# Half a step ahead instead of two slabs: when the weight sums of a Winograd MLP are queued

## The chip, the cores and the metric

The kernel runs on 8 cores of one Trainium2 chip, one batch row a core, with no exchange between cores. The metric is device time in microseconds (us) of the slowest core. The engines are named as in the profile: PE (matrix products), PEld (its weight loads), DVE (vector engine), ACT (scalar engine), POOL (GpSimd, which here issues the weight DMAs), SP (which issues the other DMAs).

## The reference

Two layers, each a token mixer and a squared-ReLU MLP with a residual add, then a final RMSNorm. x is (8, 2048, 1024) in float32.

```python
for i in range(2):
    h = rmsnorm(x, norm_mix_g[i])
    x = x + (mlstm_mixer if i == 0 else gla_mixer)(h, ...)   # chunkwise, 4 heads, chunks of 64
    h = rmsnorm(x, norm_ffn_g[i])
    x = x + square(relu(h @ ffn_w1[i])) @ ffn_w2[i]          # 1024 -> 4096 -> 1024
return rmsnorm(x, final_norm_g)
```

The change concerns the two MLPs and how their weights are prepared.

## The kernel before

Every core keeps its row of x transposed in SBUF (`xT`, 8 x 128 channels by 2048 tokens in four groups of 512) and runs in this order: mLSTM mixer, MLP of layer 0 (FFN0, some 300 to 700 us), GLA mixer, MLP of layer 1 (FFN1, from some 970 us), final norm and stores.

**The MLP.** Class `Ffn` works in steps. An "up" step makes 4 x 128 hidden columns for a pair of token groups and uses one *slab* of w1, a "down" step brings a pair of output blocks and uses two slabs of w2. A slab is 1024 x 256 weights, 1 MiB in float32, written as bf16 into one of six slots; 64 slabs a layer. Except in some last steps the product is Winograd's 2 x 2 scheme: seven block products instead of eight (1, 5, 6, 2, 3, 7, 4, in this order; `prod`), for which sums of weight blocks are needed. `Ffn.sums` makes them on DVE, four instructions a slab by `sum16` (L276): `wsum_0`, `wsum_1`, one in place in the slab, and `wsum_2`. Product 5 reads wsum_0, 6 wsum_1, 7 the sum in place and 3 wsum_2; products 1, 2 and 4 read the raw slab. An up step is 28 matmuls of 512 columns (L254), a down step 56.

**Names.** The slots' raw slabs are wraw_68, 69, 70, 71, 72 and 73 for slots 0, 1, 2, 3, 4 and 5; their first sums are wsum_0_76, 79, 82, 85, 88 and 91. In listings of orders the same tiles are wraw0_68, wsum0_0_76 and so on. `rt` or `tmp` <- `ps` at L272 (custom add-and-relu; "ISA" in listings of orders) is the eviction of products 3 and 7 out of a PSUM bank `ps`; PE can't start a product in that bank before. `Ffn.load` issues a slab's DMA on POOL's queue (L211) once PE and DVE have read the slot's last slab for the last time, which is the *gate*.

**Ticks.** While a step's products are recorded, `tick` is called after product 2 and after product 3; it runs one waiting piece of other work (`due`: norms, squares, loads of the next stage).

**What sets the order.** Instructions are not emitted as recorded. Class `Trk` records them as units with a modelled duration, and `Trk.order` simulates all engines with a list scheduler: at each step it takes, within a window of the next 48 (PE, ACT, DVE), 24 (POOL) or 4 (SP) recorded units of an engine, the one that the model can start first, the earliest recorded where several can. A DMA's landing in that model is `done[n]`, from its size and a fixed lateness; the same numbers never reach the chip. The emitted order of each engine is fixed, and semaphores hold it: an engine waits at the head of its queue.

`Ffn.run` calls `s.sums(upto)` at the start of a step, which records the sums of all slabs below `upto` that have been recorded as loaded.

Of the kernel before, what the change touches and what calls it, by code (L numbers as in the profile page):

```python
# [28 lines left out]
class Trk:  # L29
# [55 lines left out]
    def order(s):  # L85
        lastw, readers = {}, {}
        for n, u in enumerate(s.units):
            preds = set()
            for k in u["r"]:
                if k in lastw:  # L90
                    preds.add(lastw[k])
            for k0 in u["w"]:
                for k in s.ov(k0):
                    if k in lastw:
                        preds.add(lastw[k])
                    preds.update(readers.get(k, ()))
            preds.discard(n)
            u["preds"] = preds
            for k in u["r"]:
                readers.setdefault(k, []).append(n)  # L100
            for k in u["w"]:
                lastw[k] = n
                readers[k] = []
        todo = {e: [n for n, u in enumerate(s.units) if u["eng"] == e] for e in s.E}
        free = {e: 1500.0 for e in s.E}
        done, seq, hbm, xq = {}, [], 0.0, 0.0
        best = {e: None for e in s.E}
        dirty = set(s.E)
        while any(todo.values()):
            for e in s.E:  # L110
                best[e] = None
                cand = []
                held = False
                for n in todo[e][:s.WIN[e]]:
                    if s.units[n]["dma"]:
                        if held:
                            continue
                        held = True
                    rdy = 0.0
                    for p in s.units[n]["preds"]:  # L120
                        d = done.get(p)
                        if d is None:
                            rdy = None
                            break
                        pe = s.units[p]["eng"]
                        if pe == e == "pe":
                            d -= 163
                        elif s.units[p]["dma"] is None:
                            d += 206 if pe == "pe" and e == "act" else s.HOP[e]
                        rdy = max(rdy, d)  # L130
                    if rdy is None:
                        continue
                    st, safe = max(free[e], rdy), max(free[e], rdy + s.SLACK)
                    cand.append((safe, n, st))
                    if safe <= free[e]:
                        break
                if cand:
                    t0 = min(cand)[0]
                    best[e] = min((n, st) for safe, n, st in cand if safe <= t0 + 20)
            e = min((b[1], e) for e, b in best.items() if b is not None)[1]  # L140
            n, st = best[e]
            u = s.units[n]
            todo[e].remove(n)
            free[e] = st + (u["ns"] if u["dma"] else max(u["ns"] - max(s.LEAD[e], 0), 60))
            if u["dma"] and u["xp"]:
                free[e] = st + 1300
                pk = 64 if u["xp"] == "hn" else 32
                b = max(st + 1000, xq)
                slow = min(pk, int(max(0.0, hbm - b) / 200))
                xq = b + slow * 200 + (pk - slow) * 18  # L150
                done[n] = xq + 950
            elif u["dma"]:
                hbm = max(hbm, st + 1500) + u["dma"][1] / 0.29e3
                done[n] = hbm + (1200 if st < 60000 else 2500)
            else:
                done[n] = st + u["ns"] - min(s.LEAD[e], 0)
            u["st"] = st
            seq.append(n)
        s.model = max(done.values())
        return seq  # L160
# [67 lines left out]
def build():  # L228
# [22 lines left out]
    t = Trk(nc, es)  # L251
# [29 lines left out]
    def at(name, shape, dt, off=None):  # L281
        n = int(np.prod(shape[1:])) * (4 if dt == F32 else 2)
        if off is None:
            off = cur[0]
            cur[0] += (n + 31) // 32 * 32
        return nc.alloc_sbuf_tensor_at(name, list(shape), dt, offset=off), off
# [24 lines left out]
    wraw = [at("wraw%d" % i, [128, 8, 2, 128], BF16, o[0])[0] for i, o in enumerate(slots)]  # L311
# [135 lines left out]
    def nb(keep=False, full=False):  # L447
        for n in range(16):
            ring["i"] = (ring["i"] + 1) % len(ring["banks"])
            a = ring["banks"][ring["i"]]  # L450
            if a not in ring["open"] and (not full or a in ring["full"]):
                break
        else:
            assert full
            a = nb()
            mm(PB[a][:], ones_bf[:], sqb[:], [("sqb",), ("ones_bf",)], [("B", a)], True, True, True, 512)
            ring["full"].add(a)
        if keep:
            ring["open"].add(a)
        if not full:  # L460
            ring["full"].discard(a)
        return a
# [99 lines left out]
    def stats_slots(g, eng="pool"):  # L562
        return [lambda: sq_half(g, 0, eng), lambda: sq_half(g, 1, eng), lambda: sq_sum(g)]
# [14 lines left out]
    class Ffn:  # L578
# [22 lines left out]
        def load(s, gate=()):  # L601
            sl = s.slabs[s.nload]
            s.nload += 1
            i = sl["slot"]
            t.dma("pool", [(wraw[i][:].rearrange("p k a n -> p k (a n)"), sl["src"])], 1048576, r=gate,
                  w=[("wr", i), ("w3", i)], sem="slab%d" % i)

        def loads(s, used):
# [198 lines left out]
            s.loads(st["slabs"][0] - 1)  # L807

        def tick(s):
            if s.due:  # L810
                s.due.pop(0)()

        def run(s, n0, n1, hooks, late=()):
            late = list(late)
            for n in range(n0, n1):
                st = s.steps[n]
                fns = s.due = list(hooks.get(n, []))
                if n > n0 and st["kind"] != s.steps[n - 1]["kind"] or not st["wino"]:
                    for fn in late:
                        fn()  # L820
                    late = []
                    s.loads(st["slabs"][0] - 1)
                assert s.nload > st["slabs"][-1]
                s.sums(st["slabs"][-1] + 3)
                if not st["wino"]:
                    for fn in s.up_std(st)[st["done"]:]:
                        fn()
                        s.tick()
                else:
                    late = (s.up_wino if st["kind"] == "up" else s.down_wino)(st, late)  # L830
                while fns:
                    s.tick()
                s.loads(st["slabs"][0] - 1)
                if not late:
                    s.loads(st["slabs"][-1])
            for fn in late:
                fn()
            s.loads(s.steps[n1 - 1]["slabs"][-1])
# [407 lines left out]
    for k0 in range(0, KC, 2):  # L1246
        load_cols(wqk, "wqk", m_win_d, 0, 1, ks=(k0, k0 + 1))
        if k0 < 4:
# [6 lines left out]
         r=[("tri_f",)], w=[("tri_f",)], ns=400)  # L1255
# [163 lines left out]
    for k in range(KC):  # L1419
        i, n = ((1, 11 + k), (2, k - 2), (3, k - 5))[(k > 1) + (k > 4)]  # L1420
# [33 lines left out]
    for g in range(2):  # L1454
        st = stats_slots(g, "dve")
# [24 lines left out]
    for (c0, n), bank, queues in zip(PARTS, (6, 7, 5), (("sp", "sp"), ("pool", "pool"), ("sp", "act"))):  # L1480
        ts = slice(g * GS + c0, g * GS + c0 + n)
        for j in range(KC):
            a = nb()
# [5 lines left out]
            if c0:  # L1489
                t.op("pool", lambda e, j=j, ts=ts: e.tensor_scalar(  # L1490
                    out=xT[:, j, ts], in0=xT[:, j, ts], scalar1=gains[:, 32 + j:33 + j], scalar2=None, op0=ALU.mult),
                    r=[("gains",)], w=[("xT", j, g, c0)], ns=450)
# [56 lines left out]
```

How the kernel before makes its waits and increments, by code:

```python
    def _waits(s, ename, reads, writes):  # L162
        e = s.E[ename]
        pesem = s.E["pe"]["sem"]
        need = {}
        def add(sem, val):
            if ename == "pe" and sem is pesem:
                return
            if need.get(sem, 0) < val:
                need[sem] = val
        for k in reads:
            t = s.lastw.get(k)
            if t:
                add(*t)
        for k0 in writes:
            for k in s.ov(k0):
                t = s.lastw.get(k)
                if t:
                    add(*t)
                for sem, val in s.readers.get(k, {}).items():
                    add(sem, val)
        for sem, val in need.items():
            if e["waited"].get(sem, 0) < val:
                e["eng"].wait_ge(sem, val)
                e["waited"][sem] = val
# [10 lines left out]
    def emit(s):  # L197
# [11 lines left out]
                for o, i in u["dma"][0]:  # L209
                    c += 16
                    (e["eng"].dma_start_transpose if u["xp"] else e["eng"].dma_start)(out=o, in_=i).then_inc(sem, 16)
                if name:
# [15 lines left out]
def build():  # L228
# [1265 lines left out]
                act(xT[:, j, ts], xT[:, j, ts], AF.Identity, [("gains",)], [("xT", j, g, c0)], n,  # L1494
                    scale=gains[:, 32 + j:33 + j])
            if due and j > 1:
                due.pop(0)()
        rstd_fin(bank, c0, n)
        due += out_part(g, c0, n, bank, queues)
    for fn in due:
        fn()
    t.emit()
    for u in toks:
        nc.sync.wait_ge(*u["tok"])
    es.close()
    mybir.codegen_inst_isa_subclasses(nc)
    return nc
```

## Time and profile before

| | |
|---|---|
| median of 6 runs | 1381.95 us (1379.12 to 1433.39) |
| profiled execution | 1381.22 us |
| span of its slowest core | 1380.2 us |
| spans of all cores | 1372.3 to 1380.2 us, granted clock 0.990 to 0.997 |
| PE busy, slowest core | 1327.6 us, 96% |
| DVE busy | 955.8 us, 69% |
| slab DMAs and others on POOL's queue | 91.92 MB, 48.9% of the DMA engines' time |

Busy time is the union of an engine's instructions over the span. PE is the engine to look at: what it is not busy with is what another engine or a DMA can win or lose for it, so the waits of PE, and the waits of the engine that it waits for, are the views to read.

### The profile page before, as it was taken

The page shows a single profiled execution, that of the slowest core. Times are in us where ns is not written, and L with a number is a line of the kernel's source. Part 1 is how long each engine was busy: PE and PEld are TensorE (multiplying, and loading weights), DVE is VectorE, ACT ScalarE, POOL GpSimd, SP SyncE. Part 2 cuts the span into 40 slices and gives each one's busy share as a digit, 9 for nine tenths or more (in the row PEclk, how much of TensorE's full clock was granted, in tenths as well). Part 3 has the DMA queues.
Part 4 walks back from the last instruction along what each step waited for, and adds up shares of the span by engine and source line. Part 5 has one row for each costly group of instructions (what it writes and reads, how often), then busy time and mean ns, then how long its engine had stood idle before and what let it go on. Part 6 is the DMA issues. An engine that isn't in the chain of part 4 may idle for free.

```text
span 1380.2 us, 23130 instructions; the slowest of 8 cores (1372.3 to 1380.2 us)
## 1 busy us (share of the span) xinstructions
PE 1327.6 (96%) x6813; PEld 625.8 (45%) x6813; DVE 955.8 (69%) x2088; ACT 753.1 (55%) x1606; POOL 233.4 (17%) x263
## 2 busy tenths in 40 slices
PE   5999999899999999999999999999999999998997
PEld 2555554443444444444444545444444444443445
DVE  2498384967568977567658866677665888886836
ACT  2486665637158266176238765664452953942565
POOL 6021111211111111112012002050111111111114
PEclk9999999999999999999999999999999999999998
DMA  9945111368577596758674201034747857778853
GB/s 164 240 100 113 37 32 24 51 71 105 72 97 92 61 108 81 92 62 105 103 147 105 47 16 32 16 43 62 91 63 93 107 75 90 95 124 133 103 71 123
DMA packets 202011, 118.86 MB, mean 86 GB/s; under 512 B 53872, under 2 KB 187168, under 8 KB 201888
## 3 DMA queue, kind: packets, MB, share of 16 engines
q0 software_dynamic: 143392, 91.92, 48.9%
q1 hardware_dynamic: 57968, 25.20, 8.6%
q8 instruction: 57, 0.93, 0.3%
q14 instruction: 66, 0.54, 0.2%
q10 hardware_dynamic: 528, 0.26, 0.1%
HBM read 176.46 MB, written 8.39 MB: 134 GB/s over the span
## 4 chain that ended last, share of the span: by engine, by line
PE 82%; DMA 8%; DVE 4%; issue 3%; ACT 1%; POOL 1%; SPq 0%; DVEq 0%; ACTq 0%; POOLq 0%
PE ps L254 82%; DMA wraw_69<-w 2%; DMA wqk<-m_win 1%; DMA wraw_70<-w 1%; DMA wraw_72<-w 1%; DMA wraw_68<-w 1%; DMA wraw_73<-w 1%; DVE xT L264 0%; DMA xT<-m_wout 0%; DVE Cbf L1112 0%; DVE NB L988 0%; DVE R_110 L268 0%; DVE rt L272 0%; SPq L211 0%; ACT og_112 L260 0%
## 5 line engine op out<-in xcount | busy, mean ns | idle before, releaser
L260 ACT ACTIVATE ps<-ps 128x512 f32<-128x512 f32 x184 | 106.3, 584 | 190.9 <-PE ps L254 163.0
L264 DVE TENSOR_TENSOR xT<-ps,xT 128x512 f32<-128x512 f32 (+2 forms) x224 | 142.3, 647 | 95.2 <-PE ps L254 94.9
L260 ACT ACTIVATE rt<-ps 128x512 f32<-128x512 f32 x156 | 91.5, 590 | 94.1 <-PE ps L254 92.1
L260 ACT ACTIVATE sq<-xT 128x512 f32<-128x512 f32 x128 | 78.6, 626 | 29.2 <-DVE sd L264 11.6
L268 DVE SCALAR_TENSOR_TENSOR R_110<-R_110,egs,ps 128x256 f32<-128x256 f32 x112 | 52.8, 471 | 14.4 <-PE ps L254 13.4
L260 ACT ACTIVATE junk<-ps 128x256 bf16<-128x256 f32 x128 | 49.0, 383 | 25.3 <-DVE ps L264 14.2
L264 POOL TENSOR_TENSOR sd<-sd,sq 128x512 f32<-128x512 f32 x40 | 51.1, 1278 | 37.4 <-ACT sq L260 30.1
L264 POOL TENSOR_TENSOR sd<-sq 128x512 f32<-128x512 f32 x8 | 10.3, 1288 | 275.0 <-ACT sq L260 266.9
L211 POOL DMA_DIRECT2D wraw_68<-w x23 | 20.2, 878 | 196.5 <-PE ps L254 81.4
L1112 DVE TENSOR_SCALAR Cbf<-R_110,egs 128x256 bf16<-128x256 f32 x120 | 46.7, 423 | 0.9
L272 DVE CUSTOM_DVE_ANT_0 rt<-ps,rt 128x512 f32<-128x512 f32 x43 | 29.4, 685 | 22.0 <-PE ps L254 22.0
L254 PE MATMUL ps<-xn_44,wqk 128*128 128x512 bf16 x128 | 31.8, 399 | 12.6 <-DMA wqk<-m_win 12.2
L211 POOL DMA_DIRECT2D wraw_73<-w x22 | 19.3, 877 | 129.7 <-PE ps L254 69.6
L260 ACT ACTIVATE og_112<-og_112 128x512 f32<-128x512 f32 x60 | 37.6, 628 | 3.7 <-ACT og_112 L260 0.8
L211 POOL DMA_DIRECT2D wraw_69<-w x21 | 18.5, 879 | 123.0 <-PE ps L254 52.0
L260 ACT ACTIVATE og_113<-og_113 128x512 f32<-128x512 f32 x60 | 37.7, 630 | 2.7
L211 POOL DMA_DIRECT2D wraw_70<-w x19 | 16.7, 879 | 109.8 <-PE ps L254 70.8
L988 DVE TENSOR_TENSOR_SCAN NB<-ones_bf,NB 128x128 f32<-128x128 bf16 x64 | 25.4, 440 | 13.8 <-ACT NB L260 12.6
L211 POOL DMA_DIRECT2D wraw_71<-w x20 | 17.6, 880 | 99.3 <-PE ps L254 26.5
L254 PE MATMUL ps<-xn_46,wout 128*128 128x512 bf16 x128 | 29.9, 379 | 2.3 <-DVE xs_55 L268 1.3
L254 PE MATMUL ps<-wo,xn_44 128*128 128x512 bf16 x128 | 31.6, 395 | 0.0
L254 PE MATMUL ps<-xn_44,wout 128*128 128x512 bf16 x128 | 30.8, 389 | 0.8 <-ACT tiny L260 0.6
(842 smaller groups left out, 3602.0 us busy)
## 6 DMA issues: line engine op xcount, KB each, us to landing
wraw_68<-w POOLq DMA_DIRECT2D x23, 512.0 KB, 7.1
wraw_73<-w POOLq DMA_DIRECT2D x22, 512.0 KB, 7.8
wraw_69<-w POOLq DMA_DIRECT2D x21, 512.0 KB, 7.3
wraw_72<-w POOLq DMA_DIRECT2D x21, 512.0 KB, 7.6
wraw_71<-w POOLq DMA_DIRECT2D x20, 512.0 KB, 6.7
wraw_70<-w POOLq DMA_DIRECT2D x19, 512.0 KB, 8.2
outT<-xT SPq DMA_DIRECT2D x12, 512.0 KB, 6.6
xT<-xT POOLq DMA_DIRECT2D x6, 512.0 KB, 31.7
```

The costliest lines, as they stand in the source:

```text
L211: (e["eng"].dma_start_transpose if u["xp"] else e["eng"].dma_start)(out=o, in_=i).then_inc(sem, 16)
L254: t.op("pe", lambda e: e.matmul(out, lhsT=lhsT, rhs=rhs, start=start, stop=stop, **kw), r=r, w=w, sig=sig, ns=max(cols, 64) * (1.7 if f32 ...
L260: t.op("act", lambda e: e.activation(out=out, in_=in_, func=func, **kw), r=r, w=w, ns=190 + 0.84 * n + (80 if acc is not None else 0))
L264: t.op(eng, lambda e: e.tensor_tensor(out=out, in0=in0, in1=in1, op=op), r=r, w=w, ns=170 + 1.03 * n if eng == "dve" else 200 + 2.2 * n)
L268: t.op("dve", lambda e: e.scalar_tensor_tensor(out=out, in0=in0, scalar=scalar, in1=in1, op0=op0, op1=op1), r=r, w=w, ns=200 + 1.07 * n)
L272: t.op("dve", lambda e: e._custom_dve(dve_ops.TENSOR_ADD_SAT, out=out, in0=in0, in1=in1, s0=3.0e38, s1=0.0), r=r, w=w, ns=170 + 1.03 * n)
L988: t.op("dve", lambda e, cv=cv: e.tensor_tensor_scan(out=cv, data0=ones_bf[:], data1=cv, initial=0.0, op0=ALU.mult, op1=ALU.add), r=[("ones ...
L1112: t.op("dve", lambda e, h=h: e.tensor_scalar(out=Cbf[:, h, :], in0=R32[:, h, :], scalar1=ec[:, h:h + 1], scalar2=None, op0=ALU.mult), r=[( ...
```

## The change

Sums are recorded later, and the scheduler's model is told other numbers. At the start of a Winograd step only the sums up to that step's own last slab are recorded (`+1`; before, two slabs further, `+3`). The slabs of the next step are put in `s.ahead`, and each tick records the sums of one of them, ahead of the tick's other piece of work. In the model a slab's transfer takes 1150000 instead of 1048576 bytes' time, and a DMA with its own slab semaphore lands 4000 ns instead of 2500 after its modelled transfer when it starts after 60 us.

```diff
--- before.py
+++ after.py
@@ -151,7 +151,7 @@
                 done[n] = xq + 950
             elif u["dma"]:
                 hbm = max(hbm, st + 1500) + u["dma"][1] / 0.29e3
-                done[n] = hbm + (1200 if st < 60000 else 2500)
+                done[n] = hbm + (1200 if st < 60000 else 4000 if u["sem"] else 2500)
             else:
                 done[n] = st + u["ns"] - min(s.LEAD[e], 0)
             u["st"] = st
@@ -602,7 +602,7 @@
             sl = s.slabs[s.nload]
             s.nload += 1
             i = sl["slot"]
-            t.dma("pool", [(wraw[i][:].rearrange("p k a n -> p k (a n)"), sl["src"])], 1048576, r=gate,
+            t.dma("pool", [(wraw[i][:].rearrange("p k a n -> p k (a n)"), sl["src"])], 1150000, r=gate,
                   w=[("wr", i), ("w3", i)], sem="slab%d" % i)
 
         def loads(s, used):
@@ -807,6 +807,8 @@
             s.loads(st["slabs"][0] - 1)
 
         def tick(s):
+            if s.ahead:
+                s.sums(s.ahead.pop(0) + 1)
             if s.due:
                 s.due.pop(0)()
 
@@ -821,7 +823,8 @@
                     late = []
                     s.loads(st["slabs"][0] - 1)
                 assert s.nload > st["slabs"][-1]
-                s.sums(st["slabs"][-1] + 3)
+                s.sums(st["slabs"][-1] + (1 if st["wino"] else 3))
+                s.ahead = list(s.steps[n + 1]["slabs"]) if st["wino"] and n + 1 < len(s.steps) else []
                 if not st["wino"]:
                     for fn in s.up_std(st)[st["done"]:]:
                         fn()
```

What this does to the emitted orders is shown at three places.

DVE at the start of FFN0, where slot 0's slab 6 and slot 1's slab 7 are summed. d_50 and d_51 are the semaphores of the slabs of slots 0 and 1; hid are hidden columns, whose squares and sums are made here. Before; the evictions of ps5 and ps6 stand three and four rows below the last row:

```order
L276 TENSOR_TENSOR wsum0_0_76<-wraw0_68 128x512 [waits d_50]
L272 ISA rt_121<-ps1,rt_121 128x512 [waits s_pe]
L276 TENSOR_TENSOR wsum0_1_77<-wsum0_0_76,wraw0_68 128x512 [waits s_dve]
L276 TENSOR_TENSOR hid2_62<-hid2_62 128x512 [waits s_act]
L272 ISA rt_121<-ps2,rt_121 128x512 [waits s_pe]
L276 TENSOR_TENSOR wraw0_68<-wraw0_68 128x4x128
L276 TENSOR_TENSOR wsum0_2_78<-wraw0_68,wsum0_1_77 128x512 [waits s_dve]
L276 TENSOR_TENSOR hid3_63<-hid3_63 128x512 [waits s_act]
L276 TENSOR_TENSOR wsum1_0_79<-wraw1_69 128x512 [waits d_51]
L276 TENSOR_TENSOR hid3_63<-hid3_63 128x512 [waits s_dve]
L276 TENSOR_TENSOR wsum1_1_80<-wsum1_0_79,wraw1_69 128x512 [waits s_dve]
L276 TENSOR_TENSOR wraw1_69<-wraw1_69 128x4x128
```

After; the eviction of ps1 stands two rows ahead of the first row:

```order
L272 ISA rt_121<-ps2,rt_121 128x512 [waits s_pe]
L276 TENSOR_TENSOR wsum0_0_76<-wraw0_68 128x512 [waits d_50]
L276 TENSOR_TENSOR hid3_63<-hid3_63 128x512 [waits s_act]
L276 TENSOR_TENSOR wsum0_1_77<-wsum0_0_76,wraw0_68 128x512 [waits s_dve]
L276 TENSOR_TENSOR wraw0_68<-wraw0_68 128x4x128
L276 TENSOR_TENSOR hid3_63<-hid3_63 128x512 [waits s_dve]
L276 TENSOR_TENSOR wsum0_2_78<-wraw0_68,wsum0_1_77 128x512 [waits s_dve]
L276 TENSOR_TENSOR hid3_63<-hid3_63 128x512 [waits s_dve]
L276 TENSOR_TENSOR hid3_63<-hid3_63 128x512 [waits s_act,s_dve]
L272 ISA rt_121<-ps5,tmp1_123 128x512 [waits s_pe]
L276 TENSOR_TENSOR wsum1_0_79<-wraw1_69 128x512 [waits d_51]
L272 ISA rt_121<-ps6,tmp1_123 128x512 [waits s_pe]
```

The first sum of slot 0 stood ahead of the evictions of ps1 and ps2, and now stands behind both; the first sum of slot 1 stood ahead of the evictions of ps5 and ps6 and now stands between them.

PE at the start of the GLA mixer, with its projections (wv, wqk, wo) and the small gate product z = zl x wgu. Before:

```order
L254 MATMUL ps7<-wv_49,xn2_46 128x512 [waits s_act]
L254 MATMUL ps7<-wv_49,xn2_46 128x512 x7
L254 MATMUL ps0<-wv_49,xn2_46 128x512 [waits s_act]
L254 MATMUL ps0<-wv_49,xn2_46 128x512 x7
L254 MATMUL ps7<-xn3_47,wqk_48 128x512 [waits s_act]
L254 MATMUL ps7<-xn3_47,wqk_48 128x512 x7
L254 MATMUL ps1<-zl_118,wgu_128 128x512 [waits s_dve]
L254 MATMUL ps2<-zl_118,wgu_128 128x512 [waits s_dve]
L254 MATMUL ps0<-xn3_47,wqk_48 128x512 [waits s_act]
L254 MATMUL ps0<-xn3_47,wqk_48 128x512 x7
```

After:

```order
L254 MATMUL ps2<-wo_50,xn2_46 128x512 [waits s_dve]
L254 MATMUL ps2<-wo_50,xn2_46 128x512 x7
L254 MATMUL ps0<-wv_49,xn2_46 128x512 [waits s_act]
L254 MATMUL ps0<-wv_49,xn2_46 128x512 x7
L254 MATMUL ps7<-xn3_47,wqk_48 128x512 [waits s_act]
L254 MATMUL ps7<-xn3_47,wqk_48 128x512 x7
L254 MATMUL ps0<-xn3_47,wqk_48 128x512 [waits s_act]
L254 MATMUL ps0<-xn3_47,wqk_48 128x512 x7
L254 MATMUL ps1<-zl_118,wgu_128 128x512 [waits s_dve]
L254 MATMUL ps2<-zl_118,wgu_128 128x512 [waits s_dve]
```

The z matmuls stand behind one more block of eight wqk matmuls.

DVE in FFN1 by the output stage, where the multiplies of finished token groups (xT <- xT, gains, ps7 at L268, `out_held`) lie between sums; d_53 and d_55 are the slab semaphores of slots 3 and 4. Before:

```order
L276 TENSOR_TENSOR wsum3_0_85<-wraw3_71 128x512 [waits d_53]
L268 SCALAR_TENSOR_TENSOR xT_43<-xT_43,gains_131,ps7 128x512 [waits s_dve]
L276 TENSOR_TENSOR wsum3_1_86<-wsum3_0_85,wraw3_71 128x512 [waits s_dve]
L276 TENSOR_TENSOR wraw3_71<-wraw3_71 128x4x128
L268 SCALAR_TENSOR_TENSOR xT_43<-xT_43,gains_131,ps7 128x512 [waits s_dve]
L276 TENSOR_TENSOR wsum3_2_87<-wraw3_71,wsum3_1_86 128x512 [waits s_dve]
L276 TENSOR_TENSOR wsum4_0_88<-wraw4_72 128x512 [waits d_55]
L268 SCALAR_TENSOR_TENSOR xT_43<-xT_43,gains_131,ps7 128x512 [waits s_dve]
L276 TENSOR_TENSOR wsum4_1_89<-wsum4_0_88,wraw4_72 128x512 [waits s_dve]
L276 TENSOR_TENSOR wraw4_72<-wraw4_72 128x4x128
L268 SCALAR_TENSOR_TENSOR xT_43<-xT_43,gains_131,ps7 128x512 [waits s_dve]
L276 TENSOR_TENSOR wsum4_2_90<-wraw4_72,wsum4_1_89 128x512 [waits s_dve]
```

After:

```order
L268 SCALAR_TENSOR_TENSOR xT_43<-xT_43,gains_131,ps7 128x512 [waits s_dve]
L276 TENSOR_TENSOR wsum3_1_86<-wsum3_0_85,wraw3_71 128x512 [waits s_dve]
L276 TENSOR_TENSOR wraw3_71<-wraw3_71 128x4x128
L268 SCALAR_TENSOR_TENSOR xT_43<-xT_43,gains_131,ps7 128x512 [waits s_dve]
L276 TENSOR_TENSOR wsum3_2_87<-wraw3_71,wsum3_1_86 128x512 [waits s_dve]
L268 SCALAR_TENSOR_TENSOR xT_43<-xT_43,gains_131,ps7 128x512 [waits s_dve]
L276 TENSOR_TENSOR wsum4_0_88<-wraw4_72 128x512 [waits d_55]
L268 SCALAR_TENSOR_TENSOR xT_43<-xT_43,gains_131,ps7 128x512 [waits s_dve]
L276 TENSOR_TENSOR wsum4_1_89<-wsum4_0_88,wraw4_72 128x512 [waits s_dve]
L276 TENSOR_TENSOR wraw4_72<-wraw4_72 128x4x128
L276 TENSOR_TENSOR wsum4_2_90<-wraw4_72,wsum4_1_89 128x512 [waits s_dve]
```

The first sum of slot 4 stands one multiply later, and the last multiply right behind it instead of behind two more sums and a multiply.

## Rows read from the trace of the kernel before

**Rows 1.** The cores: the slowest core and the next to it.

```profile
core 0: 1380.2 us, clock 0.993
...
core 2: 1380.1 us, clock 0.994
```

**Rows 2.** The page: busy time of each engine, slowest core.

```profile
PE 1327.6 (96%) x6813; PEld 625.8 (45%) x6813; DVE 955.8 (69%) x2088; ACT 753.1 (55%) x1606; POOL 233.4 (17%) x263
```

**Rows 3.** Stretches: length, PE, PEld, DVE, ACT, POOL, PEclk, DMA share, GB/s.

```profile
350.00:640.00 290.00, 286.97 (x1328) 129.37 (x1325) 205.05 (x443) 154.94 (x285) 42.04 (x50) 1.00 0.67 83
640.00:700.00 60.00, 59.97 (x275) 26.35 (x275) 40.30 (x83) 16.81 (x30) 8.91 (x12) 1.00 0.75 107
```

**Rows 4.** PE's waits, 300 to 700 us: in total, times, longest.

```profile
PE ps L254 <- DVE rt L272: 4.4, 4, 2.5
PE ps L254 <- DVE tmp_122 L272: 1.6, 1, 1.6
```

**Rows 5.** PE's waits, 970 to 1370 us: in total, times, longest.

```profile
PE ps L254 <- DVE xT L268: 3.4, 1, 3.4
PE ps L254 <- DVE rt L272: 2.1, 2, 1.0
PE ps L254 <- DMA wraw_71<-w: 1.9, 1, 1.9
...
PE ps L254 <- DMA wraw_69<-w: 0.6, 1, 0.6
```

**Rows 6.** Timeline, 298 to 330 us: start, length, engine, line, instruction [idle before].

```profile
301.89 0.88 POOL L211 DMA_DIRECT2D wraw_72<-w  x1 [18.04 <-PE ps L254]
...
303.62 0.90 POOL L211 DMA_DIRECT2D wraw_69<-w  x1
...
311.70 0.43 DVE L276 TENSOR_TENSOR wsum_0_88<-wraw_72 128x512 bf16<-128x512 bf16 x1 [2.75 <-DMA wraw_72<-w]
...
315.91 0.43 DVE L276 TENSOR_TENSOR wsum_0_76<-wraw_68 128x512 bf16<-128x512 bf16 x1 [1.31 <-DMA wraw_68<-w]
...
316.25 0.68 DVE L272 CUSTOM_DVE_ANT_0 rt<-ps,rt 128x512 f32<-128x512 f32 x1
...
318.35 1.02 PE L254 MATMUL ps<-xs_59,wraw_71 128*128 128x512 bf16 x4 [2.46 <-DVE rt L272]
...
320.37 0.43 DVE L276 TENSOR_TENSOR wsum_0_79<-wraw_69 128x512 bf16<-128x512 bf16 x1 [0.92 <-DMA wraw_69<-w]
...
323.94 1.02 PE L254 MATMUL ps<-xs_59,wraw_73 128*128 128x512 bf16 x4 [0.77 <-DVE rt L272]
```

**Rows 7.** Timeline of DVE and of PE, 602 to 609 us.

```profile
606.60 0.43 DVE L276 TENSOR_TENSOR wsum_0_76<-wraw_68 128x512 bf16<-128x512 bf16 x1 [0.56 <-DMA wraw_68<-w]
606.94 0.68 DVE L272 CUSTOM_DVE_ANT_0 tmp_122<-ps,rt 128x512 f32<-128x512 f32 x1
...
607.77 1.02 PE L254 MATMUL ps<-xs_59,wraw_70 128*128 128x512 bf16 x4 [1.61 <-DVE tmp_122 L272]
```

**Rows 8.** Timeline by the output stage, 1238 to 1262 us: POOL, DVE, PE.

```profile
1239.66 0.88 POOL L211 DMA_DIRECT2D wraw_72<-w  x1
...
1255.83 0.43 DVE L276 TENSOR_TENSOR wsum_0_88<-wraw_72 128x512 bf16<-128x512 bf16 x1 [5.25 <-DMA wraw_72<-w]
...
1257.51 0.74 DVE L268 SCALAR_TENSOR_TENSOR xT<-xT,gains,ps 128x512 f32<-128x512 f32 x1
...
1258.39 0.38 PE L254 MATMUL ps<-hid_60,wsum_0_79 128*128 128x512 bf16 x1 [3.45 <-DVE xT L268]
```

**Rows 9.** Timeline of PE, 1336 to 1341 us.

```profile
1338.74 1.02 PE L254 MATMUL ps<-xs_59,wraw_70 128*128 128x512 bf16 x4 [1.05 <-DVE rt L272]
```

**Rows 10.** Timeline of PE at the start of the GLA mixer.

```profile
735.46 1.13 PE L254 MATMUL ps<-zl,wgu 16*128 16x512 f32 x4
...
743.93 3.61 PE L254 MATMUL ps<-xn_47,wqk 128*128 128x512 bf16 x16 [0.52 <-DVE qx_151 L268]
```

**Rows 11.** DVE's waits for slabs, whole span: costliest and least of six.

```profile
DVE wsum_0_88 L276 <- DMA wraw_72<-w: 15.8, 8, 5.3
...
DVE wsum_0_91 L276 <- DMA wraw_73<-w: 5.2, 7, 1.3
```


## The prediction

> **What bounds the kernel now.** I read the cores first, then the page's busy times, then what TensorE (PE) waits for, and last the timeline at each such wait. The profiled execution took 1381.22 us; its slowest core spans 1380.2, so 1.0 lies around the span, and it stands 0.7 below the median of 1381.95. Core 2 is only 0.1 shorter [rows 1], so a gain that holds on core 0 alone counts for nothing. PE is busy 96% of the span and no other engine more than 69% [rows 2]. In a quiet stretch of FFN0, 350 to 640 us, PE works 286.97 of 290 us at the full granted clock, 216 ns a 512-column matmul [rows 3]. So a change of order cannot win much: it can only take away PE's own waits, and PE is idle for 1380.2 − 1327.6 = 52.6 us in all.
>
> The waits that belong to weight slabs are few. From 300 to 700 us PE waits five times, 6.0 us, for the relu eviction (L272) [rows 4]. From 970 to the end it waits 3.4 for the output stage's L268, 2.1 for L272 and 2.5 for two slabs themselves [rows 5]. Two things in the rows say why an *eviction* is late:
>
> - Place A, 316 us. Three loads are issued 0.87 us apart, the first at 301.89, and their first sums run at 311.70, 315.91 and 320.37, each after VectorE (DVE) had waited for the DMA. The eviction of 316.25 stands right behind the second; PE then starts at 318.35, 2.46 late, and 0.77 late again after the third [rows 6].
> - Place D, 607 us. The sum at 606.60 waited for its slab; the eviction starts at 606.94, on its heels, and PE runs at 607.77, 1.61 late [rows 7].
>
> In the first listing of DVE's order above, wsum0_0 of slot 0 stands ahead of the evictions of ps1 and ps2, which PE had long filled. DVE runs in order, so a late slab holds two finished banks, and PE stops for lack of a bank, not for lack of a weight.
>
> At place F, by the output stage, the same thing happens with the last multiply of a group: the sum at 1255.83 waited 5.25 us for its slab, the multiply started at 1257.51 behind it, and PE at 1258.39, 3.45 late [rows 8].
>
> **The change, part by part.** It adds and removes no instruction: SP's order is the same, and POOL's differs by one mixer weight load. Nothing of a slab's DMA changes on the chip either; 1150000 and 4000 are numbers of the scheduler's model. So the price of work is 0 and everything comes from who stands behind whom.
>
> *Sums later.* In the order after, wsum0_0 stands behind both evictions of its step. The evictions then go when PE has filled their banks. What this gives, wait by wait:
>
> - A: 2.46 + 0.77 = 3.23 [rows 6]. The sum at 311.70 stays ahead of them, and wsum1_0 now stands between the evictions of ps5 and ps6, so some stays. Without the wait of the second sum, the eviction at 316.25 could go 1.31 (that wait) and 0.43 (the sum) sooner, and the second one another 0.43 (wsum0_1, which stood between): 2.17 of 2.46. Of the 0.77 I take a little: **2.3** in all.
> - B and C, two smaller ones of the same form (411 and 505 us): the L272 row of 300 to 700 has 4.4 in four, less A's 3.23, is 1.17 [rows 4, 6]: **1.1**.
> - D: the sum that waits has gone from ahead of the eviction: **1.6** [rows 7].
> - E, 984 to 993 us: PE waits 0.6 for a slab itself and once about 1.0 for L272 [rows 5]. Of the two L272 waits there, one (1338.74) has no sum near it and stays [rows 9]. The slab's load goes out sooner in the order after by several matmuls, since the wait that stalled its gate is gone: **1.6**.
> - F: 1.9 for a slab [rows 5] and 3.45 for the multiply [rows 8]. Behind the waiting sum the order after has the last multiply at once; before, one multiply and two sums stood between, 1257.51 − 1255.83 = 1.68 from the sum's start, of which 0.34 remains. That gives 1.3, and PE asks for the result two matmuls (0.4) later: 1.7. The first load is also gated 7 matmuls (1.5 us) earlier, which would give up to 1.5 more if the transfer used it. Bounds 1.7 to 3.2; I take **2.0**, near the low one, because the transfer that ends the wait runs beside output stores and took 16 us, from 1239.66 to 1255.8 [rows 8].
>
> Sum: 2.3 + 1.1 + 1.6 + 1.6 + 2.0 = **8.6**.
>
> *The cost.* DVE's sums now come nearer to their use. Counted in the orders, the shortest distance from the eviction ahead of a sum to PE's first use of it was 29 matmuls and is 14, at three places; the median falls from 85 to 77. 14 × 0.216 = 3.0 us against four sums at 0.43 [rows 6] = 1.7: cover is left, 1.3 us of it at the tightest place. I take 0. Without that cover, the three places would cost at most what the largest slab wait here cost, 3.45 each.
>
> The mixer that follows is ordered anew as well, because the model's times have moved. The four z matmuls (zl, wgu) stand one 8-matmul block later, as the second fence of orders shows; they start the chain of gates that ends in the wait of 743.93, 0.52 us today [rows 10]. A block of eight is 8 × 0.216 = 1.7. If the chain slips by 1.7 and PE's own work in front of that wait is unchanged, the wait grows by up to 1.7; the block itself isn't lost, since PE does it anyhow. Bounds: 0 (other work fills it) and 4 (the stretch 640 to 700, where PE is busy 59.97 of 60 [rows 3], opens gaps of its own as well). I take **1.5**.
>
> Net −8.6 + 1.5 = −7.1: 1381.2 − 7.1 = 1374.1 for the profiled execution, and with the 0.7 to the median **1374.8**.
>
> **A rule weighed.** Whether the slabs' transfers could be the bound themselves: at A three loads land 4.2 and 4.5 us apart [rows 6], and PE needs 28 × 0.216 = 6.05 for the products of a slab [rows 3], so transfers have a third in hand; the DMA engines are 0.67 busy there [rows 3], which says the same.
> The Trainium skill, DMA: Bandwidth & Descriptors, section Bandwidth, lists 6.15 us (341 GB/s) for a transfer of 1 MB issued from GpSimd. By that figure a slab would take longer than its products, PE would follow the transfers, and the change would save nothing. The trace's spacing of 4.2 to 4.5 us differs from it, and the measurement decides.
>
> **The rivals.**
>
> 1. *The waits are the transfers', and slip along.* Loads are gated by PE's last use of a slot, so an earlier PE asks earlier, but the DMA lands when it can. A's spacing of 4.2 to 4.5 in bursts speaks for it, and the 16 us of F; the third in hand speaks against. The stalls stay, the mixer costs 1.5: 1381.95 + 1.5 = **1383.5**. 0.15.
> 2. *More goes away.* F loses all 5.3 instead of 2.0, A all 3.2, and the mixer costs nothing: −8.6 − 3.3 − 0.9 = −12.8, **1369.2**. For it: F's wait is a queue behind one sum, and the order after shortens it on both sides. 0.15.
> 3. *Half of it.* F keeps its waits and the mixer costs 4: −6.6 + 4 = −2.6, **1379.3**: not told from no change. 0.11.
> 4. *Slower: a sum now stands between two evictions.* Place: the listing after, wsum1_0 between the evictions of ps5 and ps6, in each step that has such a pair. DVE waits for slabs 50 times, 62.2 us, six groups of which the costliest and the least are shown [rows 11]; of that 12.9 reaches PE (3.23 + 1.17 + 1.6 + 1.6 + 5.3, A to F), about a fifth. If 30% got through, 18.7, PE would lose 5.8 more and 1.5 in the mixer: 1381.95 + 7.3 = **1389.2**. It decides from 15.5 us (12.9 + 4.1 − 1.5), a quarter of the 62.2. Against it: the second eviction's bank is asked for later, and the sum that stood ahead of both has gone. 0.09.
>
> **How the numbers follow.** The forecast, 1374.8, gets 0.50; the rivals 0.15, 0.15, 0.11 and 0.09. About 0.3%, 4.1 us, is what a measurement of this kernel can tell from no change: faster is below 1377.8, slower above 1386.1. Faster: the forecast and rival 2, 0.65. Same: rivals 1 and 3, 0.26, of which 0.01 at rival 1's upper end goes to slower: 0.25. Slower: 0.09 + 0.01 = 0.10. The likeliest case's own range is 1372 to 1377.5, from F's bounds (−1.2) and the mixer's (−1.5 to +2.5). The range of 8 in 10 takes in rivals 2 and 3: **1368.5 to 1381.5**, leaving out rival 1's upper half and rival 4.
>
> **What would show it.** Right: PE's waits for L272 from 300 to 700 fall from 6.0 to about 1; the wait for L268 by the output stage falls below 2; DVE's waits for slabs remain in sum, but no longer with an eviction behind them; the mixer's wait at 743.93 grows to about 2; cores 2 and 3 shorten by as much as core 0. Wrong: PE waits on sums (L276), which today it doesn't; PE's waits for slabs themselves grow; or the span from 640 to 970 lengthens by more than 4.

## The result and the profile after

The changed kernel takes 1375.77 us (median of 10 runs) against 1382.47 for the kernel before (20 runs): a ratio of 0.9939, interval 0.9916 to 0.9963. The medians are of all executions, while ratios, means and the ranges of single executions leave out those in which the cores of a die ran at a lower granted clock, so a ratio isn't that of the two medians. The forecast was 1374.8. The profiled execution took 1374.1 us; its cores are these (span, granted clock):

```profile
core 0: 1364.9 us, clock 0.995
core 1: 1373.0 us, clock 0.993
core 2: 1368.6 us, clock 0.995
core 3: 1362.1 us, clock 0.997
```

Core 0, the slowest before [rows 1], is 15.3 us shorter; the slowest is now core 1. Which core is the slowest changes from execution to execution, so one core says little: the mean of the eight (the mean core, further on) went from 1376.9 us to 1367.7. The profiled execution before was a poor one in this respect; over all executions beside e1 to e4 the mean core before is 1374.1. The page of core 1 has for the engines:

```profile
PE 1327.5 (97%) x6813; PEld 627.1 (46%) x6813; DVE 956.1 (70%) x2088; ACT 756.4 (55%) x1606; POOL 234.0 (17%) x263
```

PE's busy time on the slowest core is the same to 0.1 us [rows 2]; there the gain is idle time. From the first to the last matmul on a slab of each layer, as a mean over eight cores, FFN0 went from 431.3 to 428.8 us, the GLA mixer between them from 245.3 to 246.5, and FFN1 from 425.3 to 417.9. So both MLPs gave, and the mixer took something back, more than these numbers say: one more block of eight wqk matmuls of the mixer (1.7 us) now runs ahead of FFN0's last slab matmul (173 matmuls that use no slab against 165), so some 1.7 us are FFN0's gain and the mixer's loss. In FFN1 the mean granted clock rose as well, from 0.994 to 1.000.

PE's waits from 300 to 700 us, and below them those from 970 to 1370 (total, times, longest):

```profile
PE ps L254 <- DVE rt L272: 1.1, 2, 0.7
PE ps L254 <- DVE xT L264: 0.3, 1, 0.3
...
PE ps L254 <- DMA wraw_70<-w: 2.1, 1, 2.1
PE ps L254 <- DVE rt L272: 1.4, 2, 1.0
```

The 6.0 us of late evictions in FFN0 [rows 4] are 1.1, and the wait for the output stage's multiply, 3.4 [rows 5], is gone. At place A the timeline of core 1 reads:

```profile
301.84 0.88 POOL L211 DMA_DIRECT2D wraw_72<-w  x1 [18.03 <-PE ps L254]
...
312.03 0.42 DVE L276 TENSOR_TENSOR wsum_0_88<-wraw_72 128x512 bf16<-128x512 bf16 x1 [1.34 <-DMA wraw_72<-w]
...
313.71 0.68 DVE L272 CUSTOM_DVE_ANT_0 rt<-ps,rt 128x512 f32<-128x512 f32 x1
314.65 0.68 DVE L272 CUSTOM_DVE_ANT_0 rt<-ps,rt 128x512 f32<-128x512 f32 x1
315.25 0.41 DVE L276 TENSOR_TENSOR wsum_0_76<-wraw_68 128x512 bf16<-128x512 bf16 x1
315.47 1.02 PE L254 MATMUL ps<-xs_59,wraw_71 128*128 128x512 bf16 x4 [0.49 <-DVE rt L272]
...
320.30 0.43 DVE L276 TENSOR_TENSOR wsum_0_79<-wraw_69 128x512 bf16<-128x512 bf16 x1 [0.84 <-DMA wraw_69<-w]
320.64 0.68 DVE L272 CUSTOM_DVE_ANT_0 rt<-ps,tmp_123 128x512 f32<-128x512 f32 x1
321.47 1.02 PE L254 MATMUL ps<-xs_59,wraw_73 128*128 128x512 bf16 x4 [0.66 <-DVE rt L272]
```

The loads go out within 0.1 us of those of [rows 6] and the sums of the second and third slab run at about the same time; but both evictions stand ahead of wsum_0_76, and PE loses 0.49 where it lost 2.46. The sum of slot 1 still lies ahead of an eviction and costs 0.66.

DVE's waits for slabs, whole span (two of seven rows):

```profile
DVE wsum_0_91 L276 <- DMA wraw_73<-w: 4.4, 5, 1.5
...
DVE wsum_0_88 L276 <- DMA wraw_72<-w: 1.7, 2, 1.3
```

All seven sum to 17.2 us, against the 62.2 of six rows in [rows 11]; in the mean of the eight cores, 60.8 us became 14.9. That was not forecast: DVE now comes to most sums when the slab is there.

### The profile page after: what moved, and what is told of

Same layout as the page of the kernel before. It is cut to its first block, busy times and chain, and to the rows that moved or that the text cites. A ratio compares the mean times of both kernels' runs of the same rounds, so it can differ in the third digit from the quotient of the medians.

```text
span 1373.0 us, 23119 instructions; the slowest of 8 cores (1362.1 to 1373.0 us)
## 1 busy us (share of the span) xinstructions
PE 1327.5 (97%) x6813; PEld 627.1 (46%) x6813; DVE 956.1 (70%) x2088; ACT 756.4 (55%) x1606; POOL 234.0 (17%) x263
## 4 chain that ended last, share of the span: by engine, by line
PE 88%; DMA 4%; DVE 3%; issue 3%; ACT 1%; POOL 1%; DVEq 0%; ACTq 0%; POOLq 0%; SPq 0%
PE ps L254 88%; DMA wqk<-m_win 2%; DMA wraw_69<-w 1%; DMA wraw_70<-w 1%; DVE Cbf L1115 1%; DVE R_110 L268 0%; DVE NB L991 0%; DVE xT L264 0%; DMA xn_44<-hn 0%; DVE hn L268 0%; POOL wqk L211 0%; POOL xT L1493 0%; ACT og_112 L260 0%; DVE xs_52 L268 0%; DVE ps L264 0%
## 5 line engine op out<-in xcount | busy, mean ns | idle before, releaser
L260 ACT ACTIVATE sq<-xT 128x512 f32<-128x512 f32 x128 | 78.7, 627 | 35.2 <-DVE sd L264 17.2
L268 DVE SCALAR_TENSOR_TENSOR R_110<-R_110,egs,ps 128x256 f32<-128x256 f32 x112 | 52.8, 472 | 18.5 <-PE ps L254 17.5
L211 POOL DMA_DIRECT2D wraw_68<-w x23 | 20.2, 877 | 201.1 <-PE ps L254 82.1
L1115 DVE TENSOR_SCALAR Cbf<-R_110,egs 128x256 bf16<-128x256 f32 x120 | 49.5, 445 | 1.2 <-PE ps L254 0.3
L211 POOL DMA_DIRECT2D wraw_73<-w x22 | 19.3, 878 | 120.5 <-PE ps L254 73.5
L211 POOL DMA_DIRECT2D wraw_69<-w x21 | 18.5, 879 | 117.8 <-PE ps L254 48.5
L211 POOL DMA_DIRECT2D wraw_70<-w x19 | 16.7, 878 | 111.5 <-PE ps L254 81.5
L211 POOL DMA_DIRECT2D wraw_71<-w x20 | 17.7, 886 | 97.4 <-PE ps L254 25.3
L211 POOL DMA_DIRECT2D wraw_72<-w x21 | 18.5, 880 | 76.5 <-PE ps L254 18.0
```

Of the source, the lines that this page charges most:

```text
L211: (e["eng"].dma_start_transpose if u["xp"] else e["eng"].dma_start)(out=o, in_=i).then_inc(sem, 16)
L260: t.op("act", lambda e: e.activation(out=out, in_=in_, func=func, **kw), r=r, w=w, ns=190 + 0.84 * n + (80 if acc is not None else 0))
L268: t.op("dve", lambda e: e.scalar_tensor_tensor(out=out, in0=in0, scalar=scalar, in1=in1, op0=op0, op1=op1), r=r, w=w, ns=200 + 1.07 * n)
L1115: t.op("dve", lambda e, h=h: e.tensor_scalar(out=Cbf[:, h, :], in0=R32[:, h, :], scalar1=ec[:, h:h + 1], scalar2=None, op0=ALU.mult), r=[( ...
```

## The experiments

Theory M: the model's later landings place the sums, whatever lead they are recorded with. Its rival S: the recording half a step ahead does it, as the change is worded. A third theory, L, is on where the time goes: all that the change wins back is what late slabs cost in front of evictions.

**One edit alone.** e1 takes the model's numbers back in the changed kernel:

```diff
-                done[n] = hbm + (1200 if st < 60000 else 4000 if u["sem"] else 2500)
+                done[n] = hbm + (1200 if st < 60000 else 2500)
-            t.dma("pool", [...], 1150000, r=gate,
+            t.dma("pool", [...], 1048576, r=gate,
```

> The changed kernel with the model's two old numbers (1048576 bytes, 2500 ns); only the recording of sums half a step ahead is left of the change. Theory M (the model's numbers carry the gain: the list scheduler places the sums by their modelled landing, whenever they were recorded): no change from before, 1382.5 within 0.3% (1378 to 1386.5), DVE's waits for slabs near 62 us on the slowest core, PE's slab waits near 13 us. Theory S (the later recording carries the gain, as the change is worded): near the changed kernel, 1375.8 within 3.

Measured: 1389.39 us, ratio 1.0038, interval 1.0017 to 1.0060; slower than before by 0.4%, which neither theory had. The mean over cores and executions is what it was (1374.5, before 1374.1), but the slowest core averages 1386.4 against 1380.6. In its profile, core 0:

```profile
PE ps L254 <- DVE rt L272: 9.0, 7, 2.5
PE ps L254 <- DMA wraw<-w: 3.8, 1, 3.8
```

DVE waits 56.2 us for slabs there. The late evictions are still there, and one slab is later for PE itself. S falls. Why the slowest cores went beyond before isn't settled: the executions at 1387 to 1391 weren't the profiled one; their slowest cores show granted clocks of 0.989 to 0.993.

e2 is the other half, the kernel before with the two new numbers:

```diff
-                done[n] = hbm + (1200 if st < 60000 else 2500)
+                done[n] = hbm + (1200 if st < 60000 else 4000 if u["sem"] else 2500)
-            t.dma("pool", [...], 1048576, r=gate,
+            t.dma("pool", [...], 1150000, r=gate,
```

> The kernel before with the model's two new numbers (1150000 bytes, 4000 ns for slabs) and sums recorded two slabs ahead as before. Theory M: near the changed kernel, 1375.8 within 3, DVE's waits for slabs below 25 us. Theory S: near before, 1382.5 within 3, DVE's waits for slabs near 62.

Measured: 1379.02 us, ratio 0.9981 (0.9967 to 0.9995): a gain, but a third of the whole; in the mean core, 1371.0 us, it is about half. DVE's slab waits are up to 38.4 us on a core. So M fails here too: it asked for 1378.8 at most and waits below 25. Its slowest core, 6, lost most at one place of its timeline:

```profile
1272.41 0.42 DVE L276 TENSOR_TENSOR wsum<-wraw 128x512 bf16<-128x512 bf16 x1 [6.47 <-DMA wraw<-w]
...
1273.58 3.57 PE L254 MATMUL ps<-xs,wraw 128*128 128x512 bf16 x8 [6.35 <-DVE rt L272]
```

The stretches around it (length, busy times of the engines, PEclk, DMA share, GB/s) are:

```profile
1240.00:1260.00 20.00, 19.07 (x88) 8.50 (x89) 16.50 (x32) 4.53 (x8) 1.78 (x3) 1.00 1.05 177
1260.00:1280.00 20.00, 13.55 (x52) 5.61 (x53) 7.30 (x18) 7.57 (x14) 2.63 (x3) 0.83 0.91 104
```

A sum ahead of an eviction again, at a place where the DMA engines are 0.91 to 1.05 busy, and PE's clock falls behind the wait.

e3 drops the lead altogether in the changed kernel:

```diff
-                s.ahead = list(s.steps[n + 1]["slabs"]) if st["wino"] and n + 1 < len(s.steps) else []
+                s.ahead = []
```

> The changed kernel with no lead in recording at all: the sums of a step's own slabs are recorded at its start and none at its ticks. Theory M: the scheduler still draws them forward within its window, so within 3 us of the changed kernel, 1375.8. Theory S: with half a step less lead PE waits on sums (L276): by product 5, the second of a step; 0.5 us at a third of 116 slabs would be 20 us, so 1385 or more.

Measured: 1374.45 us, ratio 0.9943 (0.9922 to 0.9964), the changed kernel's. So half a step of lead is worth nothing. But e2 and e3 differ in the lead alone, two slabs against none, and their executions don't meet: 1375.6 to 1382.4 us in e2, 1373.3 to 1375.4 in e3, with mean cores of 1371.0 and 1368.6. So recording the sums later gives nothing without the numbers (e1), and with them 2.5 us in the mean core and 4.6 in the median of the slowest: the gain needs both edits.

**How late the model may be.** e4 and e8 change one number of the changed kernel, e8 to 6000 and e4 to 8000:

```diff
-                done[n] = hbm + (1200 if st < 60000 else 4000 if u["sem"] else 2500)
+                done[n] = hbm + (1200 if st < 60000 else 8000 if u["sem"] else 2500)
```

> The changed kernel with 8000 instead of 4000 ns of lateness for slabs in the model. Theory M: the distance from a slab's gate to its deadline grows further, so PE's remaining slab waits (2 to 4 us in the changed kernel) go; the z matmuls of the GLA mixer stand one block earlier again, so its 1.2 us come back: 1372 (1369 to 1375). Rival (sums now too late, PE waits on L276): 1378 or more.

Measured: 1387.26 us, ratio 1.0039 (1.0025 to 1.0053). DVE hardly waits for slabs any more (6.3 us at most on a core), yet FFN0 is 440.5 to 440.8 us long on all cores, 12 more than in the changed kernel, through PE's waits there (265 to 705 us of core 6):

```profile
PE ps L254 <- ACT ps L260: 4.1, 7, 0.9
PE ps L254 <- DVE xT L264: 1.5, 2, 0.9
```

and 16 more mixer matmuls (3.5 us) that were moved ahead into it, by which the mixer got no shorter. The scheduler, told that sums come late, puts PE's products in another order, in which PE waits for ACT's copies of a bank; which products these are wasn't taken apart. Theory M's 1372 was missed by 15 us, and the rival was right in sign, not in its place (L276). The mixer's wait (L996) did not go either, 2.6 to 4.5 us on each core.

> The changed kernel with 6000 instead of 4000 ns of lateness for slabs in the model; with 8000 it was slower than before, through short waits of PE for ACT's copies that stood in all cores alike. If that cost grows evenly with the lateness: 1380 (half way between 4000 and 8000). If it comes only when the sums reach PE's first use: as with 4000 or better, 1372 to 1376.

Measured: 1376.38 us, ratio 0.9922 (0.9896 to 0.9947). Beside e5 to e8 the kernel before averaged 1386.9 us, 5 us more than beside the other runs, for a reason that isn't known, so the ratios of these four are too good; by its time e8 ends within 2 us of the changed kernel (1375.8, later 1374.5). Its cores are more alike: the mean core is 4 us longer (1372.7 against 1368.2 and 1368.8), and in each PE's waits for ACT's copies (0.6 us in the changed kernel) are 4.6. FFN0 is 433.1 to 433.3 us on every core (428.8 in the changed kernel's mean), FFN1 417.1 in the mean (417.9). The cost neither grows evenly nor is it free at 6000.

**Late slabs by themselves.** e5 is the kernel before, e6 the changed one, each with half loads from a layer's seventh slab on, so that both leave out half of these weights; the model's bytes and with them all orders are unchanged:

```diff
+            h = 4 if sl["prev"] >= 0 else 8
-            t.dma("pool", [(wraw[i][:].rearrange("p k a n -> p k (a n)"), sl["src"])], 1048576, r=gate,
+            t.dma("pool", [(wraw[i][:].rearrange("p k a n -> p k (a n)")[:, 0:h], sl["src"][:, 0:h])], 1048576, r=gate,
```

> The kernel before, same orders on every engine, but from the seventh slab of each layer on only half of a slab's weights is loaded (the other half keeps the old contents of the slot), so slabs land early. Theory L (the loss of before is evictions and products held up by late slabs): PE's slab waits of some 13 us on the slowest core go, and with them what the clock loses behind them: 1370 (1367 to 1373). Rival O (the order after is better whenever the slabs land, since evictions stand further ahead): it stays above 1376.

> The changed kernel with the same half loads from the seventh slab of each layer on. Theory L: only what is left of late slabs goes (2 to 4 us), 1371 (1368 to 1374), so nothing is left of the change's gain when both load half, and the kernel before may even be ahead by the mixer's 1 to 2 us. Rival O: faster than the kernel before with half loads by 4 us or more.

Measured: e5 1370.52 us, ratio 0.9885 (0.9855 to 0.9915); e6 1371.67, ratio 0.9890 (0.9862 to 0.9919). The slabs land in 4.3 us at the median of e5, and the two orders end together. So L holds and rival O falls: with slabs in time the order after is worth nothing, and its mean core is 2.0 us behind (1366.6 to 1364.6), which points at the mixer. Half loads also take a third off the bytes of POOL's queue (62.0 of 91.9 MB), so other transfers may gain too; that isn't separated here.

**The mixer.** e7 keeps the changed kernel, but gives the last four slabs of layer 0 the old lateness, so that PE enters the mixer in the order of before:

```diff
-                done[n] = hbm + (1200 if st < 60000 else 4000 if u["sem"] else 2500)
+                done[n] = hbm + (1200 if st < 60000 else u.get("late", 2500))
-                  w=[("wr", i), ("w3", i)], sem="slab%d" % i)
+                  w=[("wr", i), ("w3", i)], sem="slab%d" % i)["late"] = 4000 if s.L or s.nload <= 60 else 2500
```

> The changed kernel, with the model's old 2500 ns for the last four slabs of layer 0 alone. That gives PE the order of before in the GLA mixer's start and leaves both MLPs' orders as after the change. If the mixer's reordering costs what the trace shows (a wait of 2.88 us for the decays, L996, in all cores, where before it waited 0.52 for qx): that wait is gone and the median falls by 1 to 3 us against the changed kernel, 1373 (1371 to 1375). Rival: the mixer's wait only moves to another place, and the median stays at 1375 to 1376.

Measured: 1370.16 us, ratio 0.9875 (0.9839 to 0.9911). That is below its range, but the kernel before took 5 us more than elsewhere there, and the changed kernel wasn't run beside it. e9 to e12 were measured together:

> The changed kernel itself, once more, beside the next three on the same chip: the ratio to before should repeat its 0.994 within 0.002.

> The changed kernel with the model's old 2500 ns for the last four slabs of layer 0, once more. If the mixer's reordering costs the changed kernel its wait of 2.88 us for L996 and what the clock loses behind it: a ratio 0.002 to 0.003 below the changed kernel's, about 0.991. Rival (the first comparison was between chips): the same ratio as the changed kernel, within 0.001.

Measured: the changed kernel (e9) 1374.51 us, ratio 0.9957 (0.9942 to 0.9971), which repeats the first; with the old tail (e10) 1371.26, ratio 0.9921 (0.9897 to 0.9944). The difference of the medians is 3.3 us, that of the mean cores 3.6, and the executions don't meet (1373.6 us and more, 1371.8 and less). In the profiled executions the emitted orders of the two differ from 648 to 757 us alone. In the first profile of the changed kernel, PE's timeline of core 1 has:

```profile
737.09 0.39 PE L254 MATMUL ps<-qT,kT 128*128 128x128 bf16 x4
740.36 0.38 PE L254 MATMUL ps<-vt_105,ktok_102 128*128 128x256 bf16 x2 [2.88 <-DVE egs L996]
```

and its stretches are:

```profile
720.00:740.00 20.00, 17.48 (x95) 8.60 (x93) 14.72 (x36) 15.79 (x44) 2.22 (x4) 1.00 0.44 129
740.00:760.00 20.00, 19.35 (x92) 9.34 (x93) 18.38 (x33) 14.66 (x38) 9.71 (x8) 0.91 0.33 89
```

The same stretches of e10, core 1:

```profile
720.00:740.00 20.00, 19.48 (x103) 9.45 (x102) 14.44 (x38) 16.30 (x44) 1.06 (x2) 1.00 0.35 101
740.00:760.00 20.00, 19.91 (x111) 10.25 (x110) 19.58 (x39) 17.23 (x45) 10.56 (x9) 1.00 0.44 94
```

and of its waits of PE, whole span:

```profile
PE ps L254 <- DVE qx L268: 1.0, 2, 0.5
```

The wait of 2.88 us stands in all eight cores of the changed kernel and in none of e10, where the 0.5 for qx of before is back.

**The lead once more, with the mixer's order held.** e11 is e10 with e3's edit, no lead. e12 is e10 with the lead of before:

```diff
-            if s.ahead:
-                s.sums(s.ahead.pop(0) + 1)
...
-                s.sums(st["slabs"][-1] + (1 if st["wino"] else 3))
-                s.ahead = list(s.steps[n + 1]["slabs"]) if st["wino"] and n + 1 < len(s.steps) else []
+                s.sums(st["slabs"][-1] + 3)
```

> The same with no lead in recording: a step's sums are recorded at its start, none at the ticks. Theory M (with the new numbers the scheduler places the sums itself; half a step of lead in recording is worth nothing): the ratio of the run before it, within 0.001. Theory S: slower by more than 0.003.

> The same with the sums recorded two slabs ahead, as before the change; the mixer's order is the same in all three, so only the lead differs. Theory M alone: the ratio of the two runs before it, within 0.001. If the recording carries a part of its own (without the old tail, the new numbers alone gave 0.998 and both edits 0.994): slower than them by 0.002 to 0.004.

Measured: e11 1371.62 us, ratio 0.9933 (0.9908 to 0.9957); e12 1374.33, ratio 0.9948 (0.9928 to 0.9969). No lead is as good as half a step. Two slabs of lead are worse by 2.7 us in the median and 2.4 in the mean core (1367.5 against 1365.1 for both others), with overlapping intervals. By itself that is only probable; but e2 and e3 gave the same 2.5 in the mean core, and there the executions don't meet.

## Why the prediction was right, and where only by balance

The forecast was −7.1 us, the result −6.7 by the medians (−8.4 by the ratio). Its parts:

- **PE's waits are all there is to win.** Right on the slowest core, where PE's busy time stayed; and with half loads the gain has gone from the comparison (e5, e6). But over the eight cores a part of it is clock: in the two MLPs together PE's idle time fell by 8.7 us in the mean, and what a granted clock below 1.00 costs, worked out as its shortfall times the stretch, by 2.8. The sum had no term for that.
- **A to D.** Right in place and size on the slowest core. 1.15 remains at A (0.49 + 0.66; forecast 0.9), B to D are gone.
- **E.** Wrong on the slowest core: the step that the slab's load goes out sooner, so that PE no longer waits for one. PE now waits for slot 2's slab instead of slot 1's, in the timeline of core 1:

```profile
975.45 0.88 POOL L211 DMA_DIRECT2D wraw_70<-w  x1
...
991.09 0.42 DVE L276 TENSOR_TENSOR wsum_0_82<-wraw_70 128x512 bf16<-128x512 bf16 x1 [2.89 <-DMA wraw_70<-w]
...
988.01 1.02 PE L254 MATMUL ps<-xs_59,wraw_73 128*128 128x512 bf16 x4 [0.34 <-DVE rt L272]
991.13 1.86 PE L254 MATMUL ps<-xs_52,wraw_70 128*128 128x512 bf16 x4 [2.10 <-DMA wraw_70<-w]
```

Four loads are issued within 2.6 us there, as before, and the second took 15.6 us to land (12.1 before, 977.64 to 989.70). Three of the eight cores wait for a slab itself (1.5 to 2.1 us over the span); before, six did (0.9 to 4.1).

- **F.** Too small: I kept 3.3 of 5.3 us because the transfer beside the output stores might not use its earlier gate. The sum that waited 5.25 [rows 8] did not wait:

```profile
1238.09 0.87 POOL L211 DMA_DIRECT2D wraw_71<-w  x1 [7.40 <-PE ps L254]
1240.17 0.87 POOL L211 DMA_DIRECT2D wraw_72<-w  x1 [1.21 <-DVE xT L264]
...
1251.40 0.41 DVE L276 TENSOR_TENSOR wsum_0_88<-wraw_72 128x512 bf16<-128x512 bf16 x1
1251.74 0.74 DVE L268 SCALAR_TENSOR_TENSOR xT<-xT,gains,ps 128x512 f32<-128x512 f32 x1
```

The earlier gate was slot 3's, whose load goes out 1.4 us earlier against PE's work; slot 4's goes out 2.1 us behind it instead of 0.9. But slot 4's slab landed in 8.8 us (7.9 to 9.7 over the cores), where it had taken 16.1 on core 0 and 15.2 on core 2 (10.3 to 12.4 on the others). These two cores alone had waited over 3 us for the multiply. Why the transfer got shorter isn't shown.

- **The sums together.** Forecast −8.6. With the mixer's order of before (e10) the gain is 1381.15 − 1371.26 = 9.9. What the missing 1.3 are made of isn't taken apart: F's 3.3 and E's miss work against each other, and the clock of the first point comes on top.
- **The mixer.** The mechanism was right, the chain of gates starts later, and it ends in a wait; the term was mis-sized, 1.5 for 3.3. The wait that grew is the one for the decays (L996, 2.88), not that for qx (0.52, [rows 10]): 2.4 more. The rest is the clock: from 740 to 760 us five of the eight cores of the profiled execution show a granted clock between 0.91 and 0.97, against 1.00 in all eight before and in e10. On core 1, 0.09 of 20 us is 1.8. Other dips lie elsewhere in the mixer in every run; over the whole mixer and in the mean of the cores, e9 has 2.5 us more of PE's idle time than e10 and 0.9 more lost to the clock, 3.3 together. I had priced a wait at its own length.
- **DVE's waits for slabs remain in sum.** Wrong: 62.2 became 17.2 (see the profile after). A sum that stands later waits less, for its slab lands meanwhile; I had let the wait move with it.
- **Which edit.** The prediction put the new order down to sums being recorded later. That step is wrong: alone it made the kernel slower (e1), and the model's numbers alone gave a third (e2). Both are needed; of the recording it matters that it isn't two slabs ahead (e2 against e3, e12 against e10), not that it is half a step.

Rival 1 fell at A, where the loads went out no sooner and PE yet waited 0.49 instead of 2.46. The 0.67 busy share of the DMA engines held against it there is that of 350 to 640 us; around A (298 to 330) it was 0.85. Rival 2 was true of F, not of the mixer. Rival 4's place exists (0.66 at 321.47) at a quarter of what A cost. So the time was met in part by luck: 1.3 too little at the sums and 1.8 too little at the mixer nearly cancel.

The best kernel of the study is the changed one with the old tail (e7, e10): 0.9921 of before and, side by side, 3.3 us under the changed kernel.

## What to carry to other kernels

In a queue that runs in order, an instruction that waits for a transfer is priced by what stands behind it: look first for a finished bank that cannot be evicted, not for a product that lacks its weights. Where a scheduler sets the order, its assumed landing time is a tuning knob that can be set too early and too late: too early puts such waits ahead of evictions, too late bends the order of the engine that bounds (with the sums recorded late, 2500 ns gave 1.004 of before, 4000 gave 0.994, 8000 gave 1.004), and every turn also reorders stages that it was not meant for, so look at those. Try two edits that act on one order together as well as apart. When the time is that of the slowest of eight cores, look at the mean as well: e1 had the mean of before and a slowest core 6 us longer, e8 nearly the slowest core of the changed kernel and a mean 4 us longer.

## What the runs showed of the hardware

A wait of PE can cost more than its length. Behind the 6.35 us at 1273.58 in e2, eight matmuls took 3.57 us, some 0.43 each where 0.216 is usual, which is the lower of the clock's two levels; the granted clock of that stretch was 0.83. Behind the 2.88 us wait in the mixer the clock fell in five cores of eight and stayed in three, with the same instructions ahead of it in all of them; in e9, five of eight again, but not the same five. The same transfer, slot 4's slab beside the output stores, took 10.3 to 16.1 us over the eight cores of one execution before.
